# Attention scores: the pass with the low part of Q as two 64-row matmuls on the two halves of the rows, one for each half of the keys

## The reference

```python
q = rmsnorm(q.reshape(b, s, H_B, HEAD_DIM), qn_g)
k = rmsnorm(k.reshape(b, s, KV_HEADS, HEAD_DIM), kn_g)
q = apply_axial_rope(q, tables); k = apply_axial_rope(k, tables)
def attend(qblk):                      # 128 queries
    sc = jnp.einsum('bqkgd,bskd->bkgqs', qblk, k).astype(jnp.float32) * HEAD_DIM ** -0.5
    p = jax.nn.softmax(sc, axis=-1).astype(v.dtype)
    return jnp.einsum('bkgqs,bskd->bqkgd', p, v)
```

## Time and profile before

| | us |
|---|---|
| median of 3 runs | 2579.26 |
| runs | 2575.0 to 2579.67 |
| the profiled execution | 2577.73 |
| its span, first to last instruction | 2575.9 |
| first and last start of L766 | 299.8 and 1140.1 |
| PE busy | 2373.3 (92%) |
| DVE busy | 1102.1 (43%) |
| ACT busy | 905.6 (35%) |
| mean granted TensorE clock | 0.957 |

### The profile page before, as it was taken

How to read it: one execution, slowest core, us unless ns; L and a number is a source line. 1 busy time by engine, 2 the same in 40 slices (tenths; PEclk the granted TensorE clock), 3 DMA queues, 4 the chain that set the end, 5 groups by cost and what they waited for, 6 DMA issues and landing times. The chain is left out here.

```text
span 2575.9 us, 28866 instructions
## 1 busy us (share of the span) xinstructions
PE 2373.3 (92%) x11732; PEld 1975.8 (77%) x11732; DVE 1102.1 (43%) x1439; ACT 905.6 (35%) x1447; POOL 342.2 (13%) x285
## 2 busy tenths in 40 slices
PE   6999899998799989999689989989899999989997
PEld 6888688876788868887558866878688888868886
DVE  3322488825332268871713235132433333342433
ACT  4121477734221267762524012123322222222323
POOL 1087100002119510000300010002100000000001
PEclk8999899999799989999779989999899999999999
DMA  4111000014311100001311110104211111102211
GB/s 165 49 50 49 1 1 1 1 50 147 92 49 50 33 1 1 1 28 64 122 35 49 49 41 1 33 33 134 89 49 49 49 49 49 41 30 84 74 49 74
DMA packets 101969, 129.76 MB, mean 50 GB/s; under 512 B 11558, under 2 KB 64982, under 8 KB 101862
## 3 DMA queue, kind: packets, MB, share of 16 engines
q1 hardware_dynamic: 101862, 128.27, 15.6%
HBM read 111.48 MB, written 16.78 MB: 50 GB/s over the span
## 5 line engine op out<-in xcount | busy, mean ns | idle before, releaser
L186 PE MATMUL ps<-w_hi,hT_hi 128*128 128x512 f32 (+1 forms) x1408 | 539.6, 383 | 16.1 <-DVE hT_lo L224 9.9
L187 PE MATMUL ps<-w_lo,hT_hi 128*128 128x512 f32 (+1 forms) x1408 | 537.9, 382 | 0.0
L188 PE MATMUL ps<-w_hi,hT_lo 128*128 128x512 f32 (+1 forms) x1408 | 537.7, 382 | 0.0
L176 DVE TENSOR_TENSOR w_lo<-w_raw,w_hi 128x2048 fp32r<-128x2048 f32 (+1 forms) x83 | 168.8, 2034 | 790.8 <-ACT w_hi L166 788.3
L166 ACT ACTIVATE w_hi<-w_raw 128x2048 fp32r<-128x2048 f32 (+1 forms) x88 | 149.4, 1697 | 641.1 <-PE ps L188 641.1
L186 PE MATMUL ps<-hT_hi,w_hi 128*128 128x512 f32 x832 | 324.5, 390 | 4.1 <-PEq L88 3.7
L187 PE MATMUL ps<-hT_lo,w_hi 128*128 128x512 f32 x832 | 324.2, 390 | 0.0
L188 PE MATMUL ps<-hT_hi,w_lo 128*128 128x512 f32 x832 | 324.1, 390 | 0.0
L186 PEld LDWEIGHTS ps<-w_hi,hT_hi 128*128 128x128 f32 x1408 | 268.2, 190 | 69.3 <-DVE hT_lo L224 10.6
L187 PEld LDWEIGHTS ps<-w_lo,hT_hi 128*128 128x128 f32 x1408 | 268.2, 190 | 50.2
L188 PEld LDWEIGHTS ps<-w_hi,hT_lo 128*128 128x128 f32 x1408 | 267.9, 190 | 50.2
(11 more groups left out here) (187 smaller groups left out, 3203.5 us busy)
## 6 DMA issues: line engine op xcount, KB each, us to landing
w_raw<-in_w_in SPq DMA_DIRECT2D x22, 1024.0 KB, 5.1
w_raw<-in_ffn_w_up SPq DMA_DIRECT2D x44, 512.0 KB, 5.0
x_mid<-O SPq DMA_DIRECT2D x24, 512.0 KB, 5.1
w_raw<-in_gla_w_in SPq DMA_DIRECT2D x12, 1024.0 KB, 5.2
w_raw<-in_ffn_w_down SPq DMA_DIRECT2D x22, 512.0 KB, 3.6
w_raw<-in_w_out SPq DMA_DIRECT2D x8, 1024.0 KB, 5.7
xin<-x_mid SPq DMA_DIRECT2D x16, 512.0 KB, 4.2
X<-in_x SPq DMA_DIRECT2D x8, 512.0 KB, 7.8
```

Source lines behind the costliest of these rows:

```text
L176: engine.tensor_tensor(self.p.w_lo[:, slot, 0:size], self.p.w_raw[:, slot, 0:size], plane(self.p.w_hi[:, slot, 0:size]), ALU.subtract).the ...
L186: nc.tensor.matmul(out, a_hi, b_hi, start=first, stop=False)
L187: nc.tensor.matmul(out, a_hi, b_lo, start=False, stop=False)
L188: return nc.tensor.matmul(out, a_lo, b_hi, start=False, stop=last)
```

## The change

For each step the two matmuls with `QT_lo` on 128 rows are replaced by two on 64 rows: one with rows 0 to 63 of `QT_lo` and of `KT_st` for the first 512 keys, and one with rows 64 to 127 of `QT_lo` and of `KT_hi` for the last 512 keys. Both leave out Qlo·Klo. The two matmuls with `QT_hi` stay as they are and now stand together before them. `KT_hi` gets room for both key heads, a wait of ACT (for DVE's previous subtraction, on the third and fourth piece of the keys) goes, and five small tiles move to other addresses. `s_ready` is raised once for each bank, and DVE waits for both.

```diff
-    KT_hi = prog.at("KT_hi", [P, SEQ], 24, F32R)
-    nmx = prog.at("nmx", [P, 64], 28)
...
-    OT = prog.at("OT", [P, 2, 2 * P], 29)
+    KT_hi = prog.at("KT_hi", [P, KV, SEQ], 24, F32R)
+    nmx = prog.at("nmx", [P, 64], 62)
...
+    OT = prog.at("OT", [P, 2, 2 * P], 60)
...
+                group = head // (H_B // KV)
+                tok = slice(t * P, (t + 1) * P)
                 for half in range(2):
-                    keys = KT_st[:, head // (H_B // KV), half * 512:(half + 1) * 512]
-                    out = prog.ps[:, 2 * (n % 2) + half, :]
-                    nc.tensor.matmul(out, QT_hi[:, head % 2, t * P:(t + 1) * P], keys, start=True, stop=False)
-                    mm = nc.tensor.matmul(out, QT_lo[:, head % 2, t * P:(t + 1) * P], keys, start=False, stop=True)
-                mm.then_inc(s_ready, 1)
+                    nc.tensor.matmul(prog.ps[:, 2 * (n % 2) + half, :], QT_hi[:, head % 2, tok],
+                                     KT_st[:, group, half * 512:(half + 1) * 512], start=True, stop=False)
+                nc.tensor.matmul(prog.ps[:, 2 * (n % 2), :], QT_lo[0:HD, head % 2, tok],
+                                 KT_st[0:HD, group, 0:512], start=False, stop=True).then_inc(s_ready, 1)
+                nc.tensor.matmul(prog.ps[:, 2 * (n % 2) + 1, :], QT_lo[HD:P, head % 2, tok],
+                                 KT_hi[HD:P, group, 512:SEQ], start=False, stop=True).then_inc(s_ready, 1)
...
-                if i >= 2:
-                    act.wait_ge(lo_done, i - 1)
-                nc.scalar.activation(KT_hi[HD:P, cols], prog.ps[HD:P, turn_bank(i), :], ACT.Copy).then_inc(hi_done, 1)
+                nc.scalar.activation(KT_hi[HD:P, i // 2, cols], prog.ps[HD:P, turn_bank(i), :], ACT.Copy).then_inc(hi_done, 1)
...
-                    dve.wait_ge(s_ready, n + 1)
+                    dve.wait_ge(s_ready, 2 * n + 2)
```

More of the change, by code:

```diff
@@ L679, in attention @@
     KT_st = prog.at("KT_st", [P, KV, SEQ], 16, F32R)
-    KT_hi = prog.at("KT_hi", [P, SEQ], 24, F32R)
-    nmx = prog.at("nmx", [P, 64], 28)
-    sm = prog.at("sm", [P, 64], 28.25)
-    inv = prog.at("inv", [P, 64], 28.5)
-    pair_ident = prog.at("pair_ident", [P, HD], 28.75)
-    OT = prog.at("OT", [P, 2, 2 * P], 29)
+    KT_hi = prog.at("KT_hi", [P, KV, SEQ], 24, F32R)
+    nmx = prog.at("nmx", [P, 64], 62)
+    sm = prog.at("sm", [P, 64], 62.25)
+    inv = prog.at("inv", [P, 64], 62.5)
+    pair_ident = prog.at("pair_ident", [P, HD], 62.75)
+    OT = prog.at("OT", [P, 2, 2 * P], 60)
     PR = prog.at("PR", [P, 3, SEQ], 32)
@@ L896, in _ @@
                                         prog.ps[HD:P, turn_bank(i), :],
-                                        plane(KT_hi[HD:P, i % 2 * 512:(i % 2 + 1) * 512]),
+                                        plane(KT_hi[HD:P, i // 2, i % 2 * 512:(i % 2 + 1) * 512]),
                                         ALU.subtract).then_inc(lo_done, 1)
```

## The result

| | before | changed |
|---|---|---|
| median of 6 runs, us | 2579.31 | 2588.89 |
| runs, us | 2575.0 to 2582.04 | 2586.5 to 2589.78 |
| span of the profiled execution, us | 2575.9 | 2587.8 |
| the two attention layers in it, us | 469.8 | 481.6 |
| the rest between PE's first and last matmul, us | 2076.6 | 2076.6 |

The ratio is 1.0039, with a 95% interval of 1.0027 to 1.0052: 7 to 13 us slower. All of the time between the two profiles lies there. The forecast had 24.4 us more; the rival "fully side by side" had 10.3 and the time of 2589.5.

The account below looks back on a forecast made before the run. PE, busy 92% of the span, was taken to set attention's pace. 104 x 0.24 = 25.0, plus 24 x 0.06 = 1.4, less 2, gave 24.4 us more: about 2603.5 for the median, range 2582 to 2620.

Parts of the forecast that it names:

- fully side by side: Rival for the score blocks: second 64-row matmul adds 0; 10.3 us more, about 2589.5; chance 0.22.
- the value for the second 64-row matmul: Score block: time it adds after the first, taken as 0.11 us between bounds of 0 and 0.215.
- 104 places: Score blocks outside the 24 QT_lo waits: each 0.24 us longer, 25.0 us in sum.
- The price of a change of shape: Two changes in each score block, 0.20 us each: about 0.09 array running empty, about 0.11 open weight load.
- The 24 places: Steps after a turned head, PE waiting for QT_lo at L803: only 0.06 us more each, 1.4 in sum.
- The 2 us back: Short odd steps: a later PE no longer waits for DVE at the transposes, some 50 x 0.04 us.
- PE as the bound: Attention: PE sets the pace, busy 36.6 us of 40, DVE behind it at 32.1.
- The clock: Attention: clock 1.00 from the tenth us on; the rival that it falls, tens to hundreds of us, had chance 0.03.
- Faster: Rival for the score blocks: change of shape free and halves overlap; about 2564, 2549 at best; chance 0.10.
- the staggered one: The forecast itself, score blocks: 64-row matmuls overlap but their weight loads follow each other; 2603.5 us, chance 0.42.

Follow-up runs that it names:

- e2: Changed kernel with both QT_lo matmuls on rows 0 to 63, the same half of the array; 2620.99 us against 2579.84 before.
- e8: Changed kernel without its second 64-row matmul, so the QT_lo pass for the last 512 keys is left out; 2588.4 us against 2580.98 before.
- e4: Changed kernel with the 64-row pair first and the two QT_hi matmuls after it; 2593.56 us against 2580.98 before.
- e5: Changed kernel with QT_hi and 64-row QT_lo matmuls alternating, four changes of shape a block; 2675.88 us against 2579.84 before.
- e10: The changed kernel run once more, unchanged; 2587.78 us against 2580.53 before.
- e1: Changed kernel with both QT_lo matmuls back on 128 rows, order hi, hi, low, low, nothing left out; 2579.01 us against 2579.84 before.
- e7: Changed kernel with three 128-row score matmuls a block, the QT_lo pass for the last 512 keys left out; 2560.02 us against 2580.98 before.
- e3: Changed kernel with scores as three 64-row pairs; for the first 512 keys Qhi·Khi taken twice, Qhi·Klo left out; 2582.03 us against 2579.84 before.
- e9: Changed kernel with scores as three 64-row pairs, all three products, two more DVE subtractions a layer; 2586.51 us against 2580.53 before.

## Why the prediction was wrong

The direction was right and the range held the time (2582 to 2620); the size was 24.4 against 9.6 (7 to 13).

- **The step that failed** is the value for the second 64-row matmul: "I take 0.11, since it is the nearest to a row." It measured 0.00 (both at 436.91), and the weight loads of the two halves start together as well. The row that I took, 0.109 between loads, is the pace of loads into one and the same part of the array; it bounds nothing on two parts. 0.11 in 104 places and in the 24 is 14 us, and without it the sum is the rival's 10.3. e2 and e8 show both ends: 0.23 on the same half, next to nothing on the other.
- **The price of a change of shape** was right in sum. Block and transposes: 1.06 us foreseen without the second 64-row matmul, against 0.99 + 0.06 = 1.05 measured. In parts, the drain was 0.09 to 0.10 as read in the linear-attention core, and the open load 0.11 for a long one, but 0.06 ahead of the transposes. Shown by the changed kernel, e4 and e5.
- **The 24 places** with a wait for `QT_lo` were mis-sized: I had 24 x (0.24 - 0.06) = 4.3 us fall into the wait; the waits shrank by 27.2 - 24.4 = 2.8 in the changed kernel, and by no more than 27.2 - 23.6 = 3.6 in e2 and e5. The time of the second change, 0.15 at most, is all that they can hide. These steps kept their length (median 0.00), where the forecast had 0.06 more and the rival 0.05 less.
- **The 2 us back** came, in the even steps behind a plain odd one and not in the odd ones that I named: they grew by 0.07 where the other even steps grew by 0.12, so 32 x 0.05 = 1.6 us.
- **PE as the bound** held. **The clock**, which I had put at no change, was 1.00 after the first 21 us of a layer in the changed kernel, but the stretches at 0.50 at the layers' starts cost it 2.7 us in the first profile and 1.5 in e10, less the 0.2 to 0.3 that these steps would have cost at the full clock. That is 2.4 us of the 11.8 and 1.3 of the 10.5, and it is in no term of my sum. At the full clock attention would have grown by some 9.3 us (an estimate from these figures), 1 less than the rival's 10.3; that the rival stands so close to the 10.5 of e10 is in part luck. The two attention layers together spent 31 us at 0.50 in the three profiled kernels without 64-row work in them (before, e1, e7), 34 to 41 in the others, and 68 in e5. The changed kernel alone had 38 and 34 in its two profiles, so a difference of 3 us says nothing; that 64-row work is the cause is not shown.
- **Faster** was priced at 15 to 30 us for a saved step without the changes; e7 gave 21. What decides, two changes against one step, came out nearly as foreseen: 0.36 to 0.23, where that rival named 0.40.
- ACT's removed wait, the moved tiles and the second semaphore raise cost nothing that can be seen: the rest of the program is 2076.6 us in both profiles, and e1, which has all three, stands at the kernel before.

I had given the right case 0.22 and the staggered one 0.42. Of three values, the two ends and one between them, I chose the one with a row, and the row was of another situation.

## What to carry to other kernels

Two 64-row matmuls on different halves of the array, into different banks, ran and loaded side by side here (0.003 us apart), so half-empty matmuls are worth pairing; but each change between a 64-row and a 128-row shape cost 0.18 to 0.21 us of an otherwise dense queue (drain 0.1, open weight load 0.06 to 0.11). Count changes against steps saved: one step of 512 columns (0.23 us) does not pay for two changes, two steps do. If changes must be, put them where a weight load lies open anyway (e3, e9) or ahead of the transposes, where 0.06 us of the load shows in place of 0.11. And when PE is only just the bound, a gain on it is paid out in part, a loss nearly in full. Read the granted clock at the start of a stage and in its midst before a difference is given to the change: in e5 the clock was a sixth of the growth.

## What the runs showed that I had not expected

- Weight loads for the two halves start together (436.91 and 436.91), while loads into one part follow each other at 0.109 us.
- Six 64-row matmuls cost no more than the changed kernel's four (e3, e9): what counts is steps and changes, not instructions.
- The open load ahead of the transposes is half of that ahead of a 512-column matmul (0.06 and 0.11). The transposes' loads are shorter, too (L777 0.14 us in the median, L766 0.19); that the one comes of the other is not shown.
- In e5, with four changes a block, the clock fell to 0.50 four times in attention, for 3.4 us each.
- Open: the medians and the profiled attention of e3 differ (+2.2 and +6.6), the rest of the program having been 2.7 us shorter in its profile. The clock is part of it: outside attention it stood at 0.50 for 167 us in the three profiles with the shortest rest (e3, e5, e8: 2070.9 to 2073.9 us), and for 181 in the two with the longest (e2, e7: 2079.0 and 2080.3); but before, with 181 too, had 2076.6. No run tells what sets these stretches.
